# Two-layer encoder trunk on one core: inside a weight block, all products with the high weights first, all with the low weights last

## What is computed

```
def trunk(x, p):
    for layer in range(DEPTH):
        h = rmsnorm(x, p['norm_w'][layer, 0])
        m = ssd_mla_mixer(h, ...) if layer % 2 == 0 else gla_mixer(h, ...)
        x = x + rmsnorm(m, p['norm_w'][layer, 1])
        h = rmsnorm(x, p['norm_w'][layer, 2])
        f = conv_ffn(h, ...)
        x = x + rmsnorm(f, p['norm_w'][layer, 3])
    return x

def conv_ffn(h, w_in, conv_w, conv_b, w_out):
    u = dwconv_centred(jnp.einsum('bsd,df->bsf', h, w_in), conv_w, conv_b)
    gate, up = jnp.split(u, 2, axis=-1)
    return jnp.einsum('bsf,fd->bsd', jax.nn.gelu(gate, approximate=True) * up, w_out)
```

## Time and profile before

| | us |
|---|---|
| median of 3 runs | 1570.83 |
| lowest and highest | 1568.60 and 1573.79 |
| the profiled execution's own time | 1573.15 |
| its span | 1571.3 |
| TensorE busy (share of the span) | 1429.5 (91%) |
| DVE, POOL, ACT busy | 781.9, 690.0, 638.2 |
| mean granted TensorE clock | 0.952 |

### The profile page before, as it was taken

One profiled execution on the slowest core, in us unless ns is written; L12 is line 12 of the kernel. 1 busy time (PEld: TensorE's weight loads), 2 busy tenths in 40 slices (PEclk: granted clock), 3 DMA queues, 4 the chain that ended last, 5 costly groups with the idle time before them and its releaser, 6 DMA issues.

```text
span 1571.3 us, 15335 instructions
## 1 busy us (share of the span) xinstructions
PE 1429.5 (91%) x6054; PEld 1107.1 (70%) x6054; DVE 781.9 (50%) x936; ACT 638.2 (41%) x934; POOL 690.0 (44%) x339
## 2 busy tenths in 40 slices
PE   6899798989969999999997699987959999999994
PEld 4678565777846777777886477876737777778883
DVE  5435596661046766676001645355066676673004
ACT  5443474543334344434222455534334434443221
POOL 5343584023553444434554443422653444435543
PEclk9999899999988999999999699998969999999998
DMA  4222000012312332232332132310212332223331
GB/s 175 76 82 90 24 1 17 31 41 67 94 54 67 94 92 86 92 94 87 99 88 88 51 87 87 92 43 1 81 41 81 94 94 91 86 93 90 94 98 53
DMA packets 34631, 117.67 MB, mean 75 GB/s; under 512 B 3840, under 2 KB 4224, under 8 KB 34560
## 3 DMA queue, kind: packets, MB, share of 16 engines
q1 hardware_dynamic: 33840, 114.63, 23.5%
q10 hardware_dynamic: 720, 2.06, 0.4%
HBM read 114.58 MB, written 2.10 MB: 74 GB/s over the span
## 4 chain that ended last, share of the span: by engine, by line
PE 44%; DVE 29%; ACT 12%; issue 3%; DMA 0%; DVEq 0%; ACTq 0%
PE bank L254 12%; PE bank L257 12%; PE bank L258 12%; DVE cbuf L458 10%; ACT cbuf L502 4%; DVE cbuf L462 4%; ACT whi L230 3%; DVE ubuf L467 2%; DVE cbuf L532 2%; DVE cbuf L364 2%; DVE xw_lo L354 2%; ACT g_hi L511 2%; ACT cbuf L508 2%; PE bank L986 2%; DVE xres L374 1%
## 5 line engine op out<-in xcount | busy, mean ns | idle before, releaser
L238 POOL TENSOR_TENSOR wlo<-raw,whi 128x1024 fp32r<-128x1024 f32 (+2 forms) x217 | 505.3, 2331 | 752.1 <-ACT whi L230 752.1
L254 PE MATMUL bank<-xw_hi,whi 128*128 128x512 f32 x1224 | 509.1, 416 | 76.7 <-DVE xw_lo L354 62.9
L257 PE MATMUL bank<-xw_lo,whi 128*128 128x512 f32 x1224 | 492.2, 402 | 0.0
L258 PE MATMUL bank<-xw_hi,wlo 128*128 128x512 f32 x1224 | 492.1, 402 | 0.0
L254 PEld LDWEIGHTS bank<-xw_hi,whi 128*128 128x128 f32 x1224 | 234.7, 192 | 170.9 <-issue 54.6
L230 ACT ACTIVATE whi<-raw 128x1024 fp32r<-128x1024 f32 (+2 forms) x217 | 221.0, 1022 | 248.2 <-DMA raw<-in_fout 131.9
L258 PEld LDWEIGHTS bank<-xw_hi,wlo 128*128 128x128 f32 x1224 | 235.0, 192 | 57.3
L257 PEld LDWEIGHTS bank<-xw_lo,whi 128*128 128x128 f32 x1224 | 235.8, 193 | 56.0 <-issue 3.9
L458 DVE SCALAR_TENSOR_TENSOR cbuf<-ubuf,par,cbuf 128x510 f32<-128x510 f32 x100 | 183.4, 1834 | 126.5 <-ACT cbuf L502 115.9
L347 DVE RECIPROCAL rstd<-ubuf 128x512 f32<-128x512 f32 x4 | 13.4, 3353 | 363.8 <-ACT ubuf L324 363.8
L254 PE MATMUL bank<-g_hi,whi 128*128 128x512 f32 x352 | 139.4, 396 | 0.0
(11 more groups left out here) (240 smaller groups left out, 1486.0 us busy)
## 6 DMA issues: line engine op xcount, KB each, us to landing
raw<-in_fin SPq DMA_DIRECT2D x88, 512.0 KB, 3.5
raw<-in_fout SPq DMA_DIRECT2D x32, 448.0 KB, 3.2
raw<-in_gin SPq DMA_DIRECT2D x25, 512.0 KB, 3.6
raw<-in_hin SPq DMA_DIRECT2D x24, 512.0 KB, 3.5
raw<-in_hout SPq DMA_DIRECT2D x16, 512.0 KB, 3.5
raw<-in_fout SPq DMA_DIRECT2D x16, 512.0 KB, 3.5
raw<-in_gout SPq DMA_DIRECT2D x8, 512.0 KB, 3.5
xres<-in_x SPq DMA_DIRECT2D x8, 256.0 KB, 6.3
```

Source lines behind the costliest of these rows:

```text
L238: nc.gpsimd.tensor_tensor(wlo[s][:, 0:n], raw[s][:, 0:n], whi[s][:, 0:n].bitcast(F32), ALU.subtract).then_inc(w_lo, 1)
L254: first = nc.tensor.matmul(out_ap, wh, ah, start=start and k == 0, stop=False)
L257: nc.tensor.matmul(out_ap, wh, al, start=False, stop=False)
L258: last = nc.tensor.matmul(out_ap, wl, ah, start=False, stop=stop and k == kts - 1)
```

## The change

The loop over tiles in `product` is split. The first loop runs the two matmuls with `whi` for every tile, with the waits for chunks where there are any; the second runs the matmul with `wlo` for every tile. The wait ahead of the block is now for `w_hi`, and the wait for `w_lo` stands ahead of the second loop. The 24 matmuls of a block, their operands, and which one increments `mm` are the same.

```
@@ product @@
             if wait:
-                pe.wait_ge(w_lo, f + 1)
+                pe.wait_ge(w_hi, f + 1)
             for k in range(kts):
                 if by_chunk is not None:
                     pe.wait_ge(sem(by_chunk[0]), of(*by_chunk) + k0 + k + 1)
                 ah, al = ck(a_hi, k0 + k), ck(a_lo, k0 + k)
-                wh, wl = whi[s][:, (w0 + k) * P:(w0 + k + 1) * P], wlo[s][:, (w0 + k) * P:(w0 + k + 1) * P]
+                wh = whi[s][:, (w0 + k) * P:(w0 + k + 1) * P]
                 first = nc.tensor.matmul(out_ap, wh, ah, start=start and k == 0, stop=False)
                 if frees_last and k == 0:
                     first.then_inc(mm, 1)
                 nc.tensor.matmul(out_ap, wh, al, start=False, stop=False)
-                last = nc.tensor.matmul(out_ap, wl, ah, start=False, stop=stop and k == kts - 1)
+            if wait:
+                pe.wait_ge(w_lo, f + 1)
+            for k in range(kts):
+                last = nc.tensor.matmul(out_ap, wlo[s][:, (w0 + k) * P:(w0 + k + 1) * P], ck(a_hi, k0 + k),
+                                        start=False, stop=stop and k == kts - 1)
```

## The result

| | us |
|---|---|
| before, median of 4 runs | 1572.31 (1568.60 to 1574.48) |
| after, median of 4 runs | 1586.78 (1585.54 to 1588.44) |
| ratio | 1.0098, 95% interval 1.0082 to 1.0114 |
| after, the profiled execution's own time and span | 1588.44, 1586.6 |

Forecast were 1583.8 (1577 to 1590) and 13.0 us more than before. Measured are 14.5 by the medians and 1.0098 x 1572.3 - 1572.3 = 15.4 by the ratio. Of the 3.0 us between 1586.8 and 1583.8, half is that the runs of the kernel before have their median at 1572.3 and not at 1570.8.

What follows compares the result with a forecast made beforehand. TensorE, busy 91% of the span, was taken as the bound, with a DVE and ACT loop pacing the `fin` stages. Tails 11.8 plus `hout` 1.2 gave 13.0 us on 1570.83: 1583.8 us, range 1577 to 1590.

Steps and rivals of the forecast that it cites:

- (a): Ordinary blocks, more than 200: same 24 matmuls, 16 weight changes before and after; cost zero.
- (b): TensorE's waits: the one for `w_lo` moves behind 16 matmuls, one for `w_hi` takes its place; cost zero.
- The bound of 17 us to either side: Ordinary blocks: 0.01 us resolution at one step of a tile, over about 1670 tiles.
- (c): First blocks of `hin`, `fin0`, `gin`, `fin1`: seven more matmuls behind the last chunk, later clock rise; together 11.8 us.
- (d): From sum of squares through DVE's loop: the tails delay `rstd`, later waits move without shrinking; tails count in full.
- the rival in which they swallow the tails: Waits behind the stage starts absorb 9.5 us; 3.5 us remain, 1574.3 us, not measurably slower; chance 0.07.
- (e): First blocks of `hout` and `gout`: a new wait delays `hout` 1.2 us; `gout` zero.
- the four rivals: Clock does not care (0.14), waits swallow it (0.07), ordinary block becomes faster (0.03), later rise in all four (0.11).
- the last: Rival for the four stages: clock rises 6.2 us after the last chunk in all, 1587.2 us; chance 0.11.

Runs made afterwards that it cites:

- e1: Kernel before with the new order in ordinary blocks only, chunk-fed first blocks keeping the old one: 1572.00 us, ratio 1.0003 to the kernel before.
- e4: Changed kernel plus a third matmul, result unread, after each of the first seven chunks in `hin`, `fin0`, `gin`, `fin1`: 1582.65 us, ratio 1.0073 to before.
- e5: Kernel before with each low-weight matmul issued four chunks late in the first blocks of `hin`, `fin0`, `gin`, `fin1`: 1574.81 us, ratio 1.0022.
- e2: Kernel before with the new order in the six chunk-fed first blocks only: 1587.66 us, ratio 1.0108 to the kernel before.
- e3: Kernel before with the new order in the first blocks of `hin`, `fin0`, `gin`, `fin1` only: 1584.69 us, ratio 1.0085 to the kernel before.
- e6: Kernel before with the second block run together with the first, chunk by chunk, in `fin0`, `gin`, `fin1`: 1565.65 us, ratio 0.9961.

## Why the prediction held, step by step

**(a), (b) Ordinary blocks and waits: zero.** Right, by e1 (0.5 us, interval -0.9 to 1.9). The bound of 17 us to either side was much too wide a worry; the count of weight changes, 16 before and after, was the better argument.

**(c) The tails of the four stages: 11.8 us.** Measured 11.2. Both halves are confirmed apart: seven matmuls at the upper clock, 1.63, against 5.29 - 3.65 = 1.64 between `gin` and `fin1` of e4 and of before, with e5 as the half dose; and the clock, 0.454 us for each us of delay. The rise after unbroken work was put at 4.4 us; it came at 4, 5.1, 3.4 and 3.9. So `fin0` was a little too low and `gin` and `fin1` a little too high. One execution is a small sample, though. The four tails sum to 17.2 and 16.5 us in the two traces with the old order throughout the first blocks (before, e1) and to 28.5, 27.2 and 27.4 in the three with the new one (changed kernel, e2, e3). Their means are 10.8 apart, and over these twelve stages the rise came 2.4 to 5.2 us after the last chunk, 3.7 on the mean. So the term was about 1 us too high. The Trainium skill says in "TensorE: Matmul & The Clock Gate", section "Why this matters for your kernels", that TensorE has to be kept busy continuously to get to the full clock. The trace agrees in direction: on the last chunks of `fin0` TensorE was busy 3.04 of 4 us, with gaps of 0.46 us, and read 0.50. It is no sharp line: in e4, with three matmuls between the same waits, the clock rose 5.95 us after the last chunk in `hin` and 5.6 before it in `gin`. One reading in the forecast is wrong too: it calls 2.99 us the upper bound of one tail and then puts `gin` and `fin1` at 3.6. The measured 3.2 and 3.3 are over that bound, because matmuls of the second block run at the lower clock as well.

**(d) The delay reaches the end in full.** Right. The waits for `mq`, `lrk` and `ubuf` are 6.6, 4.5 and 2.9 against 6.7, 4.4 and 2.9. This rules out the rival in which they swallow the tails. DVE's lateness says the same stage by stage: 6.0 us at the reciprocal of `fin0` and 6.0 at the last chunk of `gin`, 15.2 at the reciprocal of `fin1` and 15.3 at the end. e5 agrees at a quarter of the size, by its medians: 3.7 expected, 3.5 to 3.9 at the end.

**(e) `hout` 1.2: right. `gout` 0: wrong.** `hout` took 1.18 us more, by the waits that were forecast (0.6 us at chunk 5, and short ones at the next two). For `gout` the forecast said that its first block runs at the lower clock and that POOL had its last chunks ready before either order wanted them. In the trace of before the lower clock ends at 1101.7, inside the block, and the last chunk was wanted before it was there. The row that decides it, a matmul that starts 0.05 us after POOL's end, and 0.13 us later than the rate of its stream would have it, stood in the trace; I had read POOL's merged row by its start. The step that failed is that one, and its size was 1.6 us. The 1 us that (c) had too much hides part of it, and that is luck. Of the four rivals none came true. The number of the last, 1587.2, lies closer to the measured 1586.8 than the forecast does, but its mechanism isn't what happened: it had the rise 6.2 us after the last chunk in all four stages, and it came at 3.4 to 5.1.

**The range.** 1577 to 1590 held the 1586.8. The runs of the changed kernel lie within 2.9 us of each other; most of the width was for the clock's rise, which came out near the middle.

## What to carry to other kernels

When an engine is fed piece by piece, what can be done with a piece belongs next to that piece: every instruction deferred behind the last piece is paid in full, here 0.233 us each at the upper clock, even if the total work and the weights' order cost nothing in a full stream. Find the piece-wise fed blocks first (six of 217 here) and read for each how many instructions stand behind the last arrival on the way to what the next engine waits for. The same reading turned around gave 6 us: other work into the gaps, and the instruction that others wait for (the sum of squares) right behind the last piece.

## What was not expected of the hardware

The phase of the clock's rise is loose. For the same three matmuls between chunks it came between 5.9 us before the last chunk (e4, `fin1`) and 5.95 us after it (e4, `hin`), and that is worth up to 0.454 x 5.95 = 2.7 us in one stage. With six matmuls to a chunk (e6) it was up at least 3.3 us ahead of the last chunk in all three stages. And the step is 233 ns whether the weight repeats or changes every time: in the traces of the kernel before and of the changed one the means differ by 0.2 ns at most, in that of e1 by less than 1 ns (233.7 and 232.8). Each matmul has its own weight load in both cases, so this does not tell what a load costs.
